# Expert loops of a two-layer mixture on one core: two groups of 512 columns, hidden rows turned by TensorE, another order of the matrices, and 2 MB more beside the ring

## The reference

```python
def expert_choice_ffn(h, router, w_gate, w_up, w_down):
    bn, t, _ = h.shape
    cap = CAPACITY_FACTOR * t // N_EXPERTS                # 2 * 256 // 16 = 32 tokens
    aff = jax.nn.softmax(h.astype(jnp.float32) @ router.astype(jnp.float32), axis=-1)
    gate, idx = lax.top_k(jnp.swapaxes(aff, 1, 2), cap)   # every expert takes its top 32 tokens
    xs = h[bidx, idx]
    hid = jax.nn.silu(jnp.einsum('becd,edf->becf', xs, w_gate)) * jnp.einsum('becd,edf->becf', xs, w_up)
    y = jnp.einsum('becf,efd->becd', hid, w_down) * gate[..., None].astype(h.dtype)
    return jnp.zeros_like(h).at[bidx, idx].add(y)
```

## Time and profile before

| | |
|---|---|
| median of 3 runs | 2469.47 us (2466.57 to 2470.18) |
| profiled execution, its own time | 2471.72 us |
| its span | 2469.9 us |
| TensorE busy | 2188.8 us (89%), clock 0.96 on the mean |
| VectorE busy | 1244.7 us (50%) |
| ScalarE busy | 389.7 us (16%) |
| read from memory | 655.12 MB, 266 GB/s over the span |
| experts of layer 0 | from 1314.9 us to about 1776 us |
| experts of layer 1 | from 2018.3 us to the end |

### The profile page before, as it was taken

How to read it: one execution, slowest core, us unless ns; L and a number is a source line. 1 busy time by engine, 2 the same in 40 slices (tenths; PEclk the granted TensorE clock), 3 DMA queues, 4 the chain that set the end, 5 groups by cost and what they waited for, 6 DMA issues and landing times. The chain is left out here.

```text
span 2469.9 us, 43593 instructions
## 1 busy us (share of the span) xinstructions
PE 2188.8 (89%) x19420; PEld 1576.1 (64%) x19420; DVE 1244.7 (50%) x2209; ACT 389.7 (16%) x859; POOL 38.7 (2%) x69
## 2 busy tenths in 40 slices
PE   8999999999999999999999988888799996556555
PEld 8998799499987984746645645454488553222322
DVE  7987777689777885925533221222265631111111
ACT  1121101012111001134521000000232420000000
POOL 0000000000000010000000000000000000000000
PEclk9999999999999999999999999999999998887887
DMA  9655766376558555501328999999931289999996
GB/s 322 239 171 189 239 206 223 138 276 217 172 190 279 186 209 185 194 28 35 115 116 332 425 426 426 426 426 426 385 138 35 103 356 426 427 427 427 427 427 281
DMA packets 168445, 659.16 MB, mean 267 GB/s; under 512 B 8359, under 2 KB 55971, under 8 KB 143555
## 3 DMA queue, kind: packets, MB, share of 16 engines
q1 hardware_dynamic: 162576, 639.66, 66.4%
q0 software_dynamic: 5312, 16.57, 2.2%
q10 hardware_dynamic: 370, 0.15, 0.0%
HBM read 655.12 MB, written 1.23 MB: 266 GB/s over the span
## 5 line engine op out<-in xcount | busy, mean ns | idle before, releaser
L809 PE MATMUL psum<-ring,arena 128*32 128x256 f32 x5888 | 386.9, 419 | 164.9 <-DMA ring<-in_moe_w_up 89.6
L809 PEld LDWEIGHTS psum<-ring,arena 128*32 128x32 f32 x5888 | 208.3, 118 | 339.3 <-issue 142.9
L826 PE MATMUL psum<-ring,lnp 128*32 128x256 f32 x3072 | 190.6, 402 | 64.8 <-DMA ring<-in_moe_w_down 59.1
L1698 DVE TENSOR_TENSOR arena<-psum,spare 32x256 f32<-32x256 f32 (+1 forms) x124 | 68.1, 549 | 346.8 <-PE psum L826 345.6
L826 PEld LDWEIGHTS psum<-ring,lnp 128*32 128x32 f32 x3072 | 102.5, 115 | 151.7 <-issue 46.8
L1679 DVE TENSOR_TENSOR lnp<-arena,psum 128x512 f32<-128x512 f32 (+1 forms) x32 | 26.1, 815 | 337.3 <-PE psum L809 337.3
L2375 PE MATMUL psum<-ht,ring 128*128 128x128 f32 x1472 | 176.0, 279 | 2.1 <-DMA ring<-in_w_in 2.1
L2375 PEld LDWEIGHTS psum<-ht,ring 128*128 128x128 f32 x1472 | 170.9, 195 | 6.4 <-issue 6.4
L545 PE MATMUL psum<-ring,ht 128*128 128x512 f32 x320 | 140.6, 595 | 0.0
L1120 ACT ACTIVATE arena<-psum 128x512 f32<-128x512 f32 (+1 forms) x32 | 15.7, 491 | 674.7 <-PE psum L809 674.7
L2809 DVE SCALAR_TENSOR_TENSOR spare<-ring,arena,spare 128x512 f32<-128x512 f32 x168 | 113.8, 745 | 0.0
(11 more groups left out here) (547 smaller groups left out, 3228.2 us busy)
## 6 DMA issues: line engine op xcount, KB each, us to landing
ring<-in_moe_w_down SPq DMA_DIRECT2D x64, 2048.0 KB
ring<-in_moe_w_gate SPq DMA_DIRECT2D x62, 2048.0 KB
ring<-in_moe_w_up SPq DMA_DIRECT2D x60, 2048.0 KB
ring<-in_w_in SPq DMA_DIRECT2D x51, 1024.0 KB, 8.9
ring<-in_ada_w SPq DMA_DIRECT2D x48, 1024.0 KB
ring<-in_w_ffn_gate SPq DMA_DIRECT2D x22, 1024.0 KB
ring<-in_w_ffn_up SPq DMA_DIRECT2D x22, 1024.0 KB
ring<-in_w_ffn_down SPq DMA_DIRECT2D x20, 1024.0 KB
```

The lines of the kernel that those rows point to most:

```text
L809: last = mm(bank[32 * j:32 * j + 32, SPLIT * m:SPLIT * m + SPLIT], (x_last if layer else x_four)[:, k, e % 4, SLOTS * m:SLOTS * m + SLOTS] ...
L826: last = mm(bank[32 * j:32 * j + 32, SPLIT * m:SPLIT * m + SPLIT], hidT[:, e % 2, a:a + 32], slot[:, f % 4, SPLIT * j:SPLIT * j + SPLIT], ...
L1698: ins = TTo(y_four[32 * q:32 * q + 32, s0:, cols], view(bank[r, 0:width], len(src), SPLIT), gb_moe[r, s0:, cols], ALU.mult)
```

## The change

- **Two groups of 512 columns.** A block of weight rows is now multiplied in two groups of 512 output columns. In layer 0 a group holds the context and the latent rows together (64 array columns), so 2 matmuls take the place of 8; in layer 1 it holds 32, so 2 take the place of 4. Expert 0 of layer 1 keeps four groups of 256 for g and u (`quads`).
- **Hidden rows turned by TensorE.** VectorE's transpose is gone. TensorE turns the hidden rows with the identity (`turned`, four matmuls, eight for expert 0 of layer 1), and ScalarE copies them out of PSUM. These matmuls stand between the two halves of the matrix that comes next.
- **Order.** The down product of expert e moves behind the up product of e + 1 (it was there for most experts already; now for all but expert 0 of layer 1). In layer 0 the ring's first six panels are g0, u0, g1, and y0 lies beside the ring; in layer 1 they stay g0, u0, y0.
- **More beside the ring.** The first three blocks of u1 in layer 0 (1.6 MB) and the first block of y0 in layer 1 (0.5 MB) get places of their own.
- **Last matrix in pieces.** The last down matrix of a layer comes in six transfers, the last four of one block each, with a semaphore for each piece.
- **Gate rows** are spread over the partitions that are used only, in four (two) matmuls side by side into one bank; one copy instead of four (two). The filler is six matmuls instead of three (four), and one more before the gather.

```diff
-def expert_steps():
+def expert_steps(layer):
...
+    steps = [("g", 0), ("i", 0), ("u", 0), ("r", 0)]
+    for e in range(1, EXPERTS):
+        steps += [("x", e // 4)] * (e % 4 == 0) + [("y", e - 2)] * (e > 2 - (layer == 0)) + [("t", e - 1)]
+        steps += [("y", 0)] * (layer == 1 and e == 1) + [("g", e)]
+        steps += [("c", e // 4 - 1)] * (e > 1 and e % 4 == 1) + [("u", e)]
+    return steps + [("t", EXPERTS - 1), ("y", EXPERTS - 2), ("y", EXPERTS - 1), ("c", GROUPS - 1)]
...
 def besides(layer, kind, e):
-    return (kind, e) == ("u", 1) or (layer, kind, e) == (1, "g", 1)
+    return (kind, e) in ((("y", 0),) if layer == 0 else (("g", 1), ("u", 1)))
...
+    side_rows = {0: [arena[:, 2048:3072], arena[:, 3072:4096], S["spare"][:, 1024:2048]], 1: [arena[:, 3072:4096]]}
+    with_rows = {0: ("u", 1), 1: ("y", 0)}
...
-                    sp.dma_start(view(ring[:, slot, :], PANEL // D, D), rows[:, 4 * h:4 * h + 4, :]
-                                 ).then_inc(panel_in[slot], 32)
+                    dst = view(ring[:, slot, :], PANEL // D, D)
+                    a = 0
+                    if (kind, e, h) == ("y", EXPERTS - 1, 0):
+                        a = 2
+                        sp.dma_start(dst[:, 0:2, :], rows[h][:, 0:2, :]).then_inc(last_row_in[0], 16)
+                    elif (kind, e, h) == ("y", EXPERTS - 1, 1):
+                        a = 3
+                        for i in range(3):
+                            sp.dma_start(dst[:, i, :], rows[h][:, i, :]).then_inc(last_row_in[1 + i], 16)
+                    elif (kind, e, h) == with_rows[layer] + (0,):
+                        a = len(side_rows[layer])
+                    sp.dma_start(dst[:, a:4, :], rows[h][:, a:4, :]).then_inc(panel_in[slot], 32)
...
-                    for m in range(n):
-                        for j in range(4):
-                            last = mm(bank[32 * j:32 * j + 32, SPLIT * m:SPLIT * m + SPLIT],
-                                      (x_last if layer else x_four)[:, k, e % 4, SLOTS * m:SLOTS * m + SLOTS],
-                                      row[:, SPLIT * j:SPLIT * j + SPLIT],
-                                      start=k == 0 and m == 0, stop=k == KT - 1 and m == n - 1)
+                    n = 4 if quads(layer, e) else 2
+                    cols = D // n
+                    for j in range(n):
+                        last = mm(bank[w * j:w * j + w, 0:cols], (x_last if layer else x_four)[:, k, e % 4, :],
+                                  row[:, cols * j:cols * j + cols], start=k == 0, stop=k == KT - 1)
...
+            def turned(e):
...
+                        last = mm(bank[:, 2 * w * i:2 * w * i + 2 * w], hid_e[0:2 * w, e % 2, P * i:P * i + P],
+                                  ident[0:2 * w, 0:2 * w], start=True, stop=True)
...
-                V.transpose(hidT[:, e % 2, 0:width], hid).then_inc(Q["hid_ready"], 1)
...
+                for s in reversed(src):
+                    for j in range(2):
+                        cols, a = slice(HALF * j, HALF * j + HALF), w * j + SLOTS * (s - s0)
+                        ins = TTo(y_four[32 * q:32 * q + 32, s, cols], bank[a:a + 32, :], gb_moe[a:a + 32, :], ALU.mult)
```

More of the change, by code:

```diff
@@ L267, in plan_moe @@
     gather = [("x", s, m) for m in range(2) for s in src]
-    moe = [("lg",), ("afT",)] + [("gbc", s, n) for s in src for n in range(2)] + [("idx0",)] + gather
+    moe = [("lg",), ("afT",), ("gbc",), ("idx0",)] + gather
     banks.plan(f"moe{layer}", moe)
     order = []
-    for kind, e in expert_steps():
-        if kind in "guy" and besides(layer, kind, e):
-            order += [BankPlan.TICK, (kind, e)]
+    turned = []
+    for kind, e in expert_steps(layer):
+        if kind == "t":
+            turned = [("t", e)]
         elif kind in "guy":
-            order += [EV, (kind, e), R]
+            own = (kind, e) == ("y", 0) and layer == 1
+            first = BankPlan.TICK if besides(layer, kind, e) else EV
+            order += turned * own + [first] + turned * (not own) + [(kind, e)]
+            order += [] if besides(layer, kind, e) else [R]
+            turned = []
         elif kind == "i":
@@ L437, in beside_gate @@
                     sp.dma_start(side_g[k], rows[:, k, :]).then_inc(side_g_in[k // 4], 16)
-            for kind, e in rest[:3] + [("u", 1)] + rest[3:]:
-                rows = w[kind][e].rearrange("(p j) n -> p j n", p=P)
+            for kind, e in rest[:3] + [("u", 1) if layer else ("y", 0)] + rest[3:]:
+                rows = rows_of(kind, e)
                 if besides(layer, kind, e):
@@ L800, in up @@
                                 gathered(f"moe{layer}", ("x",), k // 4)
-                    if not besides(layer, kind, e):
+                    if aside:
+                        row = side_rows[layer][k]
+                    elif not besides(layer, kind, e):
                         row = slot[:, k % 4, :]
@@ L1730, in moe @@
                     weighted(e)
+                    if (layer, e) == (0, 0):
+                        ways_back()
                 elif kind == "x":
```

179 lines of the change are left out of this document (110 added, 69 removed).

## The result

The changed kernel takes 2456.27 us (median of 4 runs, 2454.61 to 2457.23), the kernel before on the same chip 2468.02: ratio 0.9948 with a 95% interval from 0.9936 to 0.9961, so 9.6 to 15.8 us faster. The profiled execution took 2454.61 us, 17.1 less than the profiled one of before.

A forecast was written before the change was run, and what follows sets the result against it. Weight transfers at 426 GB/s were taken to bound both layers' expert loops, TensorE the part between layers. 1.4 + 3.0 - 2.1 + 4.6 + 2.4 = 9.3 us won: 2460.2 against 2469.47, range 2456 to 2467.5.

The forecast's parts named there:

- Layer 0, end: 3.0: Last landing to way back in layer 0: one block and two VectorE products left, 5.5 us to 2.55, 3.0 won.
- Layer 1, end: 4.6: Behind layer 1's last landing: shorter matmuls, VectorE products and way back, at full clock; 4.6 us won.
- Layer 1, start: 2.1 lost: Layer 1's start: longer work on g1 and u1 frees no ring slot, so the seventh panel lands 2.1 us late.
- Layer 0, start: 1.4: Layer 0's start: u1 blocks beside the ring save 3.7 us, less a 2.3 us hole in the transfers; 1.4 won.
- Fewer instructions: 2.4, range 0 to 4: Both layers: fewer instruction transfers on the 16 engines, priced by their share of them; 2.4 us won, ends 0 and 4.
- At nothing: gate rows and filler: Token choice: narrow matmuls and six fillers take about 6 us as before, while VectorE picks tokens; no gain.
- the slow layer 1: Rival, 10%: layer 1's two groups lose the clock or don't run side by side, TensorE bounds; 2500 to 2640 us.
- the eaten gains: Rival, 16%: small pieces gain less and layer 1's start hole is 5 us; 2.5 us won, 2467, no difference told.
- The third: Rival, 5%: no hole at layer 0's start, none at layer 1's; 13.8 us won, 2455.7.

The follow-up runs named there:

- experts 0 and 1 in four groups: Changed kernel with four groups of 256 columns for gate and up of layer 1's experts 0 and 1, not only 0; ratio 0.9943.
- pieces of 256 and 128: Two runs: changed kernel with every weight product cut into two pieces of 256 (128) columns, ratio 0.9966, or four of 128 (64), ratio 1.0042.
- the run with filler: Kernel before with one more filler product in layer 0 and one ahead of the gather in both layers; ratio 0.9999.
- 60 waits on SyncE: Changed kernel with 60 waits that hold at once on SyncE behind each ring panel of layer 0's experts 3 to 14; ratio 0.9978.
- the waits on TensorE: Changed kernel with eight more waits that hold at once ahead of each block's matmuls, layer 0, experts 2 to 14; ratio 0.9955.

## Why the prediction was right in sign and too small

- **Layer 0, end: 3.0** measured 2.94; less up to 0.7 for pieces that land later.
- **Layer 1, end: 4.6** measured 4.51, with the clock at 1.00 as argued.
- **Layer 1, start: 2.1 lost** measured 1.6 with experts 0 and 1 in four groups, by one trace. The seventh panel went out 34.4 us behind g0, the forecast had 35.2.
- **Layer 0, start: 1.4** had the right sum for the rows, 3.7 less a hole of 2.3, but the hole with what follows it took 3.2; what is left is 0.1 us against after and 0.5 against the mean. The step left out the order: y0 behind u1 no longer stands and frees slots late. The text named the wait of y0 that goes away and priced it at nothing. In before's two traces it cost 0.4 and 1.5 us. So the whole start is worth 1.0 to 1.5 us, and that 1.4 is near it is luck: one part was too large and the other missing.
- **Fewer instructions: 2.4, range 0 to 4** is the step that failed. It took the packets' share of the 16 engines, as if the engines stood in for one another. The marks show that they don't: the packets make eight of the sixteen shares late. Layer 0's landing is 7.7 us nearer on the mean (447.4 and 439.7), and 6.2 to 6.7 of that is left when the start is taken off, for 34 packets fewer (49 and 15): 0.18 to 0.20 us each, nearly three times the 0.07 of the share. The runs with pieces of 256 and 128 give 2.9 us for 12 and 7.5 for 35 (0.24, 0.21). In layer 1 the landing is 431.8 on the mean in spite of its hole of 1.6, where before and the run with filler have 432.0; that leaves some 1.8 us for the packets there too, as a remainder. So the term was 8.0 to 8.5 us in place of 2.4.
- **At nothing: gate rows and filler** measured 1.6 us in the trace, at most 2.2 in the time. The forecast took the filler's length, and not that the gather behind it ran at a clock of 0.81 before (9.04 us) and at 1.00 after (7.41).

By traces these are 2.9 + 4.5 - 1.6 + 7.7 (start and packets of layer 0) + 1.8 + 1.6 = 16.9, less 0.8 in the mixer between the layers (its L734 took 9.61 us, before's L696 8.80): 16.1, and the profiles differ by 15.6 behind the start of the token choice. The sum closes so well in part because two of its terms are remainders. The medians differ by 12 to 13; the rest can't be assigned, since steps of 2 us are below what an interval tells.

Of the rivals, the slow layer 1 and the eaten gains did not come. The third named a time near the one measured (2455.7) by the wrong way: both holes that it denied are there.

Three things stay open. One is how layer 0's 7.7 us divide between the start and the packets more closely than above: no run has before's whole order with the new products. The second is why a packet costs its engine more than its own length. With 34 packets fewer the eight late shares came from 9.5 us behind the earlier eight to about 3, where 34 x 1.07 us over eight engines would be 4.5; with 60 waits on SyncE it is 8.6 us for 17 x 0.31 = 5.3. The third is whether the short matmuls cost something besides: the waits on TensorE, which would tell, reached only 4 packets in the loop, but they too have eight late shares.

## What to carry to other kernels

In a loop bound by transfers that fill all 16 engines, count the instructions, of every engine: what they cost is set by the shares that they make late, not by their part of the mean rate. Look at the rate in the last microseconds ahead of a landing on which all wait; a dip there means unequal engines. When a run is to bring back one part of a change, compare its order of work with before's down to the last step. And price the clock of what stands behind a filler, not the filler.

## What the runs showed of the hardware that was not expected

- An instruction packet of 16 KB took 1.07 us of one engine on the mean, where a data packet of the same size took 0.62. About 256 instructions, matmuls and weight loads counted each, make one: in the run with pieces of 128 columns 8296 in 300 us came with 32 packets. Before has 49 of them in layer 0's loop, after 15. The Trainium skill, Runtime: NRT & Kernel Launch, section Instruction fetch mechanics, says of crossing such a block that it is "one DMA tail-bump, mostly hidden". The block's size agrees; hidden it is not in this loop, with 0.18 to 0.24 us each at the last landing, and in the run with pieces of 128 columns TensorE stood 6.7 us on "issue" in two matrices.
- TensorE's instruction packets go with eight late shares of sixteen (8.1 us behind the others in before, at the last landing), SyncE's with one (8.6 us behind with 17 packets more).
- Packets of SyncE, of 8 KB, cost more each (0.3 and 0.5 us at the last landing) than those of TensorE, though they take 0.31 us of one engine. One late share against eight accounts for the direction; the size is open.
- Layer 1's loop with two groups of 32 for all products (TensorE busy 85% of the time) was granted 1.00, before's with four groups (59%) 0.81, and the run with four groups for gate and up and two for down (68%) 0.88.
